# Ranks of three token tiles computed inside the last output product, the first pair's token products dealt among the router's steps, and a first gate product that waits half by half

## The reference, cut to what matters

```python
def hier_moe(h, w_grp, b_grp, w_rt, b_rt, w_gate, w_up, w_down):
    xt = h.reshape(B * S, D)                                   # 512 x 1024
    p_g, g_sel = lax.top_k(softmax(xt @ w_grp + b_grp), 1)     # group, then two experts in it
    v2, e_sel = lax.top_k(softmax(chosen_group(xt @ w_rt + b_rt)), 2)
    gate = p_g * v2 / sum(v2)
    eid = g_sel * 8 + e_sel
    y = (silu(xb @ w_gate[e]) * (xb @ w_up[e])) @ w_down[e]    # xb: the tokens of expert e
    return sum over the two experts of y * gate

x = x + mixed @ w_out[i]
x = x + hier_moe(rms_norm(x, norm_ffn[i]), ...)
```

## Time and profile before

| | |
|---|---|
| median of 3 runs | 1466.11 us (1465.14 to 1467.55) |
| the profiled execution | 1467.75 us |
| its span, first to last instruction | 1465.8 us |
| TensorE busy | 1392.1 us, 95% of the span |
| VectorE, ScalarE, GpSimd busy | 596.7, 326.7, 100.6 us |
| read from memory | 458.46 MB, 320 GB/s over the span |
| mean granted TensorE clock | 0.987 |

### The profile page before, as it was taken

One profiled execution on the slowest core, in us unless ns is written; L12 is line 12 of the kernel. 1 busy time (PEld: TensorE's weight loads), 2 busy tenths in 40 slices (PEclk: granted clock), 3 DMA queues, 4 the chain that ended last, 5 costly groups with the idle time before them and its releaser, 6 DMA issues. The chain is left out here.

```text
span 1465.8 us, 16868 instructions
## 1 busy us (share of the span) xinstructions
PE 1392.1 (95%) x6384; PEld 628.9 (43%) x6449; DVE 596.7 (41%) x1118; ACT 326.7 (22%) x636; POOL 100.6 (7%) x195
## 2 busy tenths in 40 slices
PE   7999999999999999989899988999999999999998
PEld 3464467333333333333454555464334334333333
DVE  4654114434334333332639865144334334333334
ACT  4455012011111110111226765020101101110110
POOL 1001000200000000000000224002000000000000
PEclk9999999999999999999999999999999999999999
DMA  8207484899999999999810030777999999999994
GB/s 291 99 0 227 150 320 161 334 427 427 425 428 427 426 427 427 428 428 427 320 28 1 1 120 1 261 301 287 404 427 426 426 427 428 426 427 427 427 429 203
DMA packets 67365, 457.09 MB, mean 312 GB/s; under 512 B 15404, under 2 KB 23148, under 8 KB 43368
## 3 DMA queue, kind: packets, MB, share of 16 engines
q1 hardware_dynamic: 61248, 447.96, 74.8%
q0 software_dynamic: 5216, 8.22, 1.5%
q10 hardware_dynamic: 840, 0.06, 0.0%
HBM read 458.46 MB, written 10.53 MB: 320 GB/s over the span
## 5 line engine op out<-in xcount | busy, mean ns | idle before, releaser
L1540 PE MATMUL ps<-arena,xT 128*64 128x512 f32 x2048 | 457.6, 600 | 20.2 <-DMA arena<-in_moe_w_gate 15.2
L1540 PEld LDWEIGHTS ps<-arena,xT 128*64 128x64 f32 x2048 | 149.9, 138 | 308.2 <-issue 308.1
L2193 DVE TENSOR_TENSOR x<-ps,x 128x1024 f32<-128x1024 f32 x120 | 146.5, 1225 | 211.3 <-PE ps L1562 208.9
L1554 PE MATMUL ps<-arena,xT 128*64 128x512 f32 x1024 | 228.9, 599 | 1.8 <-ACT xT L1127 1.8
L1187 PE MATMUL ps<-xT,arena 128*128 128x512 f32 x384 | 169.0, 595 | 1.7 <-DVE xT L1702 1.3
L1562 PE MATMUL ps<-mix,xT 128*128 128x512 bf16 x660 | 157.4, 379 | 6.4 <-issue 4.6
L1554 PEld LDWEIGHTS ps<-arena,xT 128*64 128x64 f32 x1024 | 71.4, 137 | 133.6 <-issue 129.7
L1187 PE MATMUL ps<-arena,mix 128*128 128x512 f32 (+1 forms) x288 | 119.0, 570 | 0.0
L1562 PEld LDWEIGHTS ps<-mix,xT 128*128 128x128 bf16 x720 | 65.5, 98 | 119.5 <-issue 48.7
L1187 PEld LDWEIGHTS ps<-xT,arena 128*128 128x128 f32 x384 | 71.9, 190 | 91.2 <-issue 88.4
L1127 ACT ACTIVATE xT<-ps 128x512 f32<-128x512 f32 x32 | 19.1, 597 | 392.0 <-PE ps L1546 392.0
(11 more groups left out here) (276 smaller groups left out, 1141.2 us busy)
## 6 DMA issues: line engine op xcount, KB each, us to landing
arena<-in_moe_w_gate SPq DMA_DIRECT2D x64, 2048.0 KB, 28.8
arena<-in_moe_w_up SPq DMA_DIRECT2D x64, 2048.0 KB, 27.7
arena<-in_moe_w_down SPq DMA_DIRECT2D x64, 2048.0 KB, 32.6
arena<-in_w_out SPq DMA_DIRECT2D x4, 2048.0 KB, 11.2
arena<-in_dsa_w_in SPq DMA_DIRECT2D x1, 5120.0 KB, 15.8
arena<-in_lru_w_in SPq DMA_DIRECT2D x4, 1024.0 KB, 10.8
arena<-in_w_mem_kv SPq DMA_DIRECT2D x2, 2048.0 KB, 9.9
scratch_xn<-arena SPq DMA_DIRECT2D x8, 512.0 KB, 5.5
```

Source lines behind the costliest of these rows:

```text
L1540: ins = pe.matmul(ps[e * CAP:(e + 1) * CAP, bank, :], tokT[:, k, e * CAP:(e + 1) * CAP], rows_in[u][:, k, :], start=k == 0, stop=k == KD - 1)
L1554: ins = pe.matmul(ps[e * CAP:(e + 1) * CAP, BANK_Y + c, :], hT[:, j, e * CAP:(e + 1) * CAP], rows_down[u][:, j, c * 512:(c + 1) * 512], st ...
L2193: dve.tensor_tensor(x[:, t, :], ps[:, b:b + 2, :].rearrange("p a n -> p (a n)"), x[:, t, :], ALU.add).then_inc(s_, 1)
```

## The change

- In `out_order` the step `rank` moves ahead of `out 3 1`. On TensorE it now only takes the bank; the six rank matmuls are issued inside `out 3 1`, behind channel 4 of its eight. On VectorE the copy of the ranks and `first_slots` for the three tiles now stand ahead of the last output product's eviction; before, `first_slots` stood inside the step `fT 3`.
- The 24 token products of tiles 0 to 2 no longer stand together behind the router product of tile 3. Four stand ahead of the transposes of tile 3, four behind them, 13 behind the router product, and 3 behind the ranks of tile 3. `bank_ahead` waits for their two banks out of turn.
- The first gate product waits for the eviction of `first.0` ahead of slice 0 and for that of `first.1` ahead of slice 4. Before, it waited for both ahead of slice 0.

Nothing is added or removed: the matmuls, evictions and transfers are the same in number and size.

```diff
--- before.py
+++ after.py
@@ -109,7 +109,7 @@
     if L == 0:
         steps.append(("mem", 1))
     steps += [("out", 0, 1), ("out", 1, 1), ("fT", 0), ("out", 2, 1), ("fT", 1), ("route", 0), ("out", 3, 0),
-              ("fT", 2), ("route", 1), ("route", 2), ("out", 3, 1), ("rank", 0), ("fT", 3), ("route", 3)]
+              ("fT", 2), ("route", 1), ("route", 2), ("rank", 0), ("out", 3, 1), ("fT", 3), ("route", 3)]
     return steps
 
 
@@ -1179,6 +1179,13 @@
                     who = jobs.reader[n - 8]
                     pe.wait_ge(emptied[who], jobs.before[n - 8][who])
                 return ps[:, n % 8, :]
+
+            def bank_ahead(name):
+
+                n = jobs.number[name]
+                who = jobs.reader[n - 8]
+                pe.wait_ge(emptied[who], jobs.before[n - 8][who])
+                return bank(name)
 
             def product(name, pairs, cols=slice(0, 512), part=slice(0, P), close=True, b=None):
 
@@ -1459,8 +1466,29 @@
                                         start=u == 0, stop=u == t)
                     return ins
 
+                def first_tokens(k, t):
+                    return pe.matmul(b_first[k // 4][:, (k % 4) * P:(k % 4 + 1) * P], xn_ffn[:, t, k * P:(k + 1) * P],
+                                     first_hot[:, t].rearrange("p e n -> p (e n)"), start=t == 0 and k % 4 == 0,
+                                     stop=t == NT - 1 and k % 4 == 3)
+
+                three_tiles = [(k, t) for k in range(KD) for t in range(NT - 1)]
                 for what, t, *half in out_order(L):
-                    if what == "out":
+                    if what == "out" and (t, half[0]) == (NT - 1, 1):
+                        b = open_bank(f"{L}.out.{t}.1")
+                        for c in range(8):
+                            ins = pe.matmul(b, mix[:, c, t * P:(t + 1) * P], w_out[1][:, c, :], start=c == 0, stop=c == 7)
+                            if c == 4:
+                                pe.wait_ge(chosen, 3 * L + 1)
+                                for q in range(NT - 1):
+                                    ranked = ranks_of(b_rank, q, q)
+                                ranked.then_inc(filled, 1)
+                        ins.then_inc(filled, 1)
+                        b_first = [bank_ahead(f"{L}.first.{h}") for h in range(2)]
+                        pe.wait_ge(rows_normed, rows[L, "ffn", NT - 2])
+                        pe.wait_ge(first_placed, 2 * L + 1)
+                        for k, u in three_tiles[0:4]:
+                            first_tokens(k, u)
+                    elif what == "out":
                         h = half[0]
                         if h == 0:
                             wait_emptied(pe, f"{L}.xo.{t}")
@@ -1471,15 +1499,14 @@
                         wait_emptied(pe, f"{L}.out.{t}.1")
                         for h in range(2):
                             transposes(f"{L}.fT.{t}.{h}", x[:, t, :], first=4 * h)
+                        if t == NT - 1:
+                            for k, u in three_tiles[4:8]:
+                                first_tokens(k, u)
                     elif what == "mem":
                         for i in range(4):
                             memory_product(1, i)
                     elif what == "rank":
-                        b = open_bank(f"{L}.rank.0")
-                        pe.wait_ge(chosen, 3 * L + 1)
-                        for q in range(NT - 1):
-                            ins = ranks_of(b, q, q)
-                        ins.then_inc(filled, 1)
+                        b_rank = open_bank(f"{L}.rank.0")
                     else:
                         if t == 0:
                             pe.wait_ge(route_scaled, L + 1)
@@ -1487,24 +1514,18 @@
                         wait_emptied(pe, f"{L}.fT.{t}.1")
                         product(f"{L}.route.{t}", [(xT[:, k, t * P:(t + 1) * P], w_route[:, k, :]) for k in range(KD)], cols=slice(0, R))
 
+                for k, u in three_tiles[8:21]:
+                    first_tokens(k, u)
                 b_rank = open_bank(f"{L}.rank.1")
-                b_first = [open_bank(f"{L}.first.{h}") for h in range(2)]
-
-                def first_tokens(k, t):
-                    return pe.matmul(b_first[k // 4][:, (k % 4) * P:(k % 4 + 1) * P], xn_ffn[:, t, k * P:(k + 1) * P],
-                                     first_hot[:, t].rearrange("p e n -> p (e n)"), start=t == 0 and k % 4 == 0,
-                                     stop=t == NT - 1 and k % 4 == 3)
-
-                pe.wait_ge(rows_normed, rows[L, "ffn", NT - 2])
-                pe.wait_ge(first_placed, 2 * L + 1)
-                for k in range(KD):
-                    for t in range(NT - 1):
-                        first_tokens(k, t)
                 pe.wait_ge(chosen, 3 * L + 2)
                 ranks_of(b_rank, NT - 1, 0)
                 for u in range(NT):
                     ins = pe.matmul(b_rank[:, NE:2 * NE], ones_b[:], choice[:, u, :], start=u == 0, stop=u == NT - 1)
                 ins.then_inc(filled, 1)
+                for k, u in three_tiles[21:24]:
+                    first_tokens(k, u)
+                for h in range(2):
+                    open_bank(f"{L}.first.{h}")
                 pe.wait_ge(rows_normed, rows[L, "ffn", NT - 1])
                 pe.wait_ge(first_placed, 2 * L + 2)
                 for k in range(KD):
@@ -1533,9 +1554,11 @@
                         ins = pe.transpose(ps[:, BANK_XT[k // 4], (k % 4) * P:(k % 4) * P + n], xg[0:n, k::KD][:, 0:P], ident[0:n, 0:n])
                     ins.then_inc(s_, 1)
 
-                def both(bank, units, s_):
+                def both(bank, units, s_, spread=None):
 
                     for k in range(KD):
+                        if spread and k % 4 == 0:
+                            wait_emptied(pe, spread[k // 4])
                         for e, u in enumerate(units):
                             ins = pe.matmul(ps[e * CAP:(e + 1) * CAP, bank, :], tokT[:, k, e * CAP:(e + 1) * CAP], rows_in[u][:, k, :],
                                             start=k == 0, stop=k == KD - 1)
@@ -1579,10 +1602,12 @@
                     for j in (0, 1):
                         pe.wait_ge(landed[units[j]], times[j] * 16)
                     if first:
-                        wait_emptied(pe, f"{L}.first.1")
+                        for name in (f"{L}.rank.1", f"{L}.fT.{NT - 1}.0"):
+                            wait_emptied(pe, name)
+                        both(BANK_GATE, units[0:2], m["gate_psum"], [f"{L}.first.{h}" for h in range(2)])
                     else:
                         pe.wait_ge(m["xt_sbuf"], n * 2)
-                    both(BANK_GATE, units[0:2], m["gate_psum"])
+                        both(BANK_GATE, units[0:2], m["gate_psum"])
                     if first:
                         banks_emptied()
                         table()
@@ -2070,14 +2095,13 @@
                         wait_filled(dve, jn)
                         dve.tensor_copy(xT[:, 4:8, t * P:(t + 1) * P], bank(jn).rearrange("p (k n) -> p k n", k=4))\
                            .then_inc(emptied["dve"], 1)
-                        if t == NT - 1:
-                            wait_emptied(dve, f"{L}.rank.0")
-                            first_slots(0, t, ranks[:, 0:t, 0:2])
                         rows_normalise(L, "ffn", (t,), lambda t: x[:, t, :], lambda t: xn_ffn[:, t, :])
                     elif what == "rank":
                         wait_filled(dve, f"{L}.rank.0")
                         dve.tensor_copy(ranks[:, 0:NT - 1], bank(f"{L}.rank.0")[:, 0:(NT - 1) * NE].rearrange("p (t e) -> p t e", t=NT - 1))\
                            .then_inc(emptied["dve"], 1)
+                        wait_emptied(dve, f"{L}.rank.0")
+                        first_slots(0, NT - 1, ranks[:, 0:NT - 1, 0:2])
                     elif what == "route":
                         k = rows[L, "ffn", t]
                         wait_filled(dve, f"{L}.route.{t}")
```

## The result

| | before | after |
|---|---|---|
| median | 1466.83 us (4 runs, 1465.14 to 1470.06) | 1457.2 us (4 runs, 1455.89 to 1458.37) |
| the profiled execution, its span | 1467.75, 1465.8 us | 1455.89, 1454.0 us |
| mean granted clock | 0.987 | 0.994 |

The change is faster: ratio 0.9926, with a 95% interval of 0.9912 to 0.9939 (the two medians of the table alone give 0.9934, 9.6 us). The forecast was 1457.3.

The account below looks back on a forecast made before the run. TensorE and VectorE bound it up to the first gate product, which restarts the weight stream that ends each expert stage. 6.04 + 4.40 us, together 10.4 (clock 4.3, schedule 6.1), off 1467.75 gave 1457.3 us; range 1453.9 to 1462.3.

Parts of the forecast that it names:

- The sum: Gate product starts 6.04 us earlier in layer 0 and 4.40 in layer 1, together 10.4 us.
- (a): Six rank matmuls inside the last output product: delay the transposes of tile 3 by 0.13 us; choice ready 0.17 us early.
- (d): Behind tile 3's router product: with 13 token products, ranks start 7.20 us after the transposes, tile 3's token products at 8.23.
- (b): VectorE's first_slots for three tiles moves into idle time ahead of the last eviction: worth nothing, 0.56 us without ScalarE's cover.
- (c): Eight token products into the two gaps around tile 3's transposes: no delay, router product 1.98 us behind them, clock full.
- (e): First gate product's wait per half: starts 1.99 us behind tile 3's first token product, in place of 2.89.
- The clock's share: Part of the gain from the clock staying full between transposes of tile 3 and gate product: 4.3 us over both layers.
- The schedule's: Part of the gain from the reordering ahead of the gate product, without the clock: 6.1 us over both layers.
- a bound of the range: First pair of layer 1: a second clock fall that goes too would take 1.7 us more off.
- The rival of falls that stay: Clock still falls around the router product of tile 3; gain only 3.0 + 3.0 us, 1461.7; chance 0.22.

Follow-up runs that it names:

- rank_early: Changed kernel with the six rank matmuls behind the third channel of the last output product in place of the fifth; 1461.93 us.
- gaps_filled: Kernel before with seven useless matmuls added in the two waits around the transposes of tile 3, nothing moved; 1462.54 us.
- gaps_open: Changed kernel with the eight token products taken out of the two waits around the transposes and put behind the router product; 1465.94 us.
- late_stream: Changed kernel with pair 1's two down weights waiting for the end of the first up product instead of the first gate product; 1474.32 us.
- whole_wait: Changed kernel with the split taken back: the first gate product waits for both token evictions ahead of its first slice; 1459.05 us.
- second_gap_open: Changed kernel with the four token products behind the transposes of tile 3 moved behind the router product, the four ahead kept; 1461.34 us.
- split_only: Kernel before with the first gate product's wait split into two halves and nothing else; 1466.39 us.
- after_again: Changed kernel once more, unaltered; 1457.58 us.
- pair_filled: Changed kernel with seven useless matmuls added in two waits of the first pair of experts; 1455.94 us.
- waits_filled: Changed kernel with seven useless matmuls in the first pair and 25 more in three longer waits elsewhere; 1455.34 us.

## Why the prediction was right

The sum stood on one distance, from the transposes of tile 3 to the gate product. It came to 10.24 us in both layers, where 10.22 was worked out. Step by step:

- (a) The ranks, with the four token products behind them, cost 0.17 us in layer 0 (from the product's start at 234.76 to the transposes at 242.89 are 8.13 us, 7.96 before), forecast 0.13. From the choice to the ranks were 0.19 us, forecast 0.17, and the prediction called that margin. But its own (d) allows 0.14 us for a semaphore, and the ranks of tile 3 started 0.15 us behind their choice; so only 0.04 us was to spare, and that nothing had to be paid was partly luck. rank_early shows what lies on the other side. The page of the Trainium skill that speaks against this place ("TensorE: Matmul & The Clock Gate", Part 2: matmuls stay in program order) is right in the trace of rank_early, and costs nothing where the choice is early.
- (b) and (c) hold: `first_slots` in idle time, the router product 1.99 us behind the transposes (forecast 1.98), clock 1.00.
- (d) The ranks of tile 3 start 7.22 us behind the transposes (forecast 7.20), and VectorE's choice is what they wait for. Three products then cover the wait for the slots entirely.
- (e) Taken back, the split costs 1.85 us; 0.9 per layer was forecast.
- The clock's share was forecast at 4.3 us, and gaps_filled measured 4.7 (its interval is about 2.9 to 6.5); by the distances of its profile it is 3.26 + 1.62 = 4.9. The schedule's is 13.13 - 10.24 = 2.89 us per layer at full clock, 5.8 in all; 6.1 was forecast. Most of both errors comes from the price of a token product (0.24 for 0.23), and they cancel in the sum. But the two shares are not free of each other: gaps_open has the schedule without the cover and is only 1.5 us below the kernel before.
- The profiled execution fell by 11.86 us, not 10.4. The fall in the first pair of layer 1 is not in the new profile, and that stage is 1.46 us shorter. It had been kept as a bound of the range, at 1.7. The expert stages do follow their first gate product: with that of layer 0 6.03 us earlier, the transposes of layer 1 were 5.83 us earlier (983.22 and 977.39), and late_stream shows the stream's part in it.
- That the median of 1457.2 lies within 0.1 us of the forecast is luck. The sum of 10.4 us was taken from one execution of 1467.75, 0.9 us above the median of 1466.83; from median to median 9.6 us went, from profile to profile 11.86.

The rival of falls that stay stood at 0.22 and would have been 1461.7. The prediction drew from the Trainium skill ("TensorE: Matmul & The Clock Gate", "HAM oscillation", where waits of several microseconds let the clock fall) that filling shorter ones would not touch the clock. The traces of gaps_filled and gaps_open contradict that: there waits of 0.7 to 1.0 us made the difference. That the later brackets of 0.67 and 0.88 us, and rank_early's of 1.41, let nothing fall ahead of the gate shows that the length of one wait isn't the whole rule. What it is stays open.

## What to carry to other kernels

When a short wait on TensorE stands ahead of dense work, look at the granted clock behind it before pricing the wait: here two waits of 0.7 and 0.8 us per layer cost more through the clock (4.7 us over two layers) than they lasted (3.1). Moving work that has to be done anyway into them wins twice, while reordering without filling them won 1.5 us here, hardly more than can be measured. Where a stage ends on a stream of transfers, find the instruction that restarts the stream, and measure the gain there.

## What was not expected of the hardware

- The order of matmuls with 64 columns of weights that write different halves of PSUM's partitions matters: 32 records of 512 columns took 7.02 us with the two experts interleaved, 12.19 us one expert after the other, with the same weights and the same clock.
- A fall of the clock in the first pair costs its 1.7 us on TensorE, but only 0.4 us (whole_wait) to 1.1 (gaps_open) at the end of layer 0's stage, where the stream of weights sets the end. In layer 1, from the gate product to the end of the span, before, gaps_open, second_gap_open, rank_early and split_only, which have the fall, take 467.1 to 467.8 us; after, after_again, whole_wait, gaps_filled and pair_filled, which don't, take 465.6 to 466.7, and waits_filled 467.4.
- Two profiles of the same changed kernel differ by 1.7 us through one fall of the clock 120 us into the span, in a part that no edit touched; its runs lie in two groups some 2 us apart, for which this may be the reason.
